# A two-block model in one kernel: first weight units in halves, products of zeros at the start, the linear attention's decayed keys computed first

## The reference, cut to what matters

```python
n = rms_norm(h, attn_norm)                       # 512 x 1024
z = n @ w_in
gq, gk, gv, g_low, g_r, c_q, c_kv, k_r = split_cols(z, IN_SPLITS)
log_a = log_sigmoid(g_low @ gla_gate_w2 + gla_gate_b) / 16
# linear attention: 4 heads, 64 keys and 128 values wide, chunks of 64 tokens
def step(state, inp):
    qi, ki, vi, gi = inp
    b = cumsum(gi, axis=2); b_last = b[:, :, -1:, :]
    o_inter = (qi * exp(b)) @ state
    decay = exp(where(causal, b_t - b_s, -inf))
    scores = einsum('bhtk,bhsk,bhtsk->bhts', qi, ki, decay)
    k_dec = ki * exp(b_last - b)
    state = state * exp(b_last) + k_dec.T @ vi
    return state, o_inter + scores @ vi
# softmax attention: 8 heads, queries and keys 96 wide, values 64, query blocks of 128, block-causal
q_m = rms_norm(rms_norm(c_q) @ mla_w_uq); kv = rms_norm(c_kv) @ mla_w_ukv   # rotary part, norms
o_m = mla_attention(q_m, k_m, v_m)
h = h + concat([o_g, o_m]) @ w_out
# then the MLP, a gated projection, and a second block (pooling, two gated FFNs with a short
# convolution, a 16-head banded attention); none of it is touched
```

## Time and profile before

| what | value |
|---|---|
| median of 3 runs | 1713.98 us (1710.64 to 1714.53) |
| the profiled execution | 1710.77 us, its span 1709.0 us |
| PE busy | 1667.6 us (98% of the span) |
| DVE, ACT, POOL busy | 955.7, 610.6, 120.9 us |
| mean granted TensorE clock | 0.990 |

### The profile page before, as it was taken

How to read it: one execution, slowest core, us unless ns; L and a number is a source line. 1 busy time by engine, 2 the same in 40 slices (tenths; PEclk the granted TensorE clock), 3 DMA queues, 4 the chain that set the end, 5 groups by cost and what they waited for, 6 DMA issues and landing times.

```text
span 1709.0 us, 19162 instructions
## 1 busy us (share of the span) xinstructions
PE 1667.6 (98%) x8098; PEld 1348.7 (79%) x8098; DVE 955.7 (56%) x1409; ACT 610.6 (36%) x851; POOL 120.9 (7%) x103
## 2 busy tenths in 40 slices
PE   7898899999999999999999999999999999999999
PEld 5785678888888888888888888877766888888887
DVE  4767756534343465847646546655655477356453
ACT  4346533423232333523322222445655433222221
POOL 1110010000000001500000000221200200000000
PEclk9899899999999999999999999999999999999999
DMA  5220003735353622122322313322221132322221
GB/s 177 99 99 1 1 26 114 116 123 88 124 88 104 119 101 97 51 74 99 123 82 93 121 69 105 99 97 75 84 97 38 49 123 100 119 77 99 99 80 68
DMA packets 26038, 153.84 MB, mean 90 GB/s; under 512 B 3360, under 2 KB 4528, under 8 KB 9952
## 3 DMA queue, kind: packets, MB, share of 16 engines
q1 hardware_dynamic: 24048, 146.83, 24.1%
q0 software_dynamic: 1328, 4.86, 4.9%
q10 hardware_dynamic: 576, 0.92, 0.2%
HBM read 147.88 MB, written 4.72 MB: 89 GB/s over the span
## 4 chain that ended last, share of the span: by engine, by line
PE 92%; DVE 5%; ACT 2%; issue 0%; DMA 0%; ACTq 0%
PE bank L517 24%; PE bank L519 24%; PE bank L518 24%; PE bank L523 4%; PE bank L525 3%; PE bank L524 3%; PE bank L1097 1%; PE bank L1119 1%; PE bank L1106 1%; DVE WL L1516 1%; PE bank L705 1%; PE bank L743 1%; ACT WH L1163 1%; ACT tmp L1300 1%; PE bank L726 0%; PE bank L983 0%
## 5 line engine op out<-in xcount | busy, mean ns | idle before, releaser
L517 PE MATMUL bank<-AH,WH 128*128 128x512 f32 (+1 forms) x1152 | 453.0, 393 | 12.3 <-DVE WL L1516 12.3
L518 PE MATMUL bank<-AL,WH 128*128 128x512 f32 (+1 forms) x1184 | 462.7, 391 | 0.0
L519 PE MATMUL bank<-AH,WL 128*128 128x512 f32 (+1 forms) x1152 | 449.9, 391 | 0.0
L1516 DVE TENSOR_TENSOR WL<-RAW,WH 128x2048 fp32r<-128x2048 f32 (+1 forms) x136 | 307.2, 2261 | 180.3 <-ACT WH L1163 180.3
L1163 ACT ACTIVATE WH<-RAW 128x2048 fp32r<-128x2048 f32 (+1 forms) x136 | 253.8, 1868 | 259.8 <-PE bank L519 238.7
L517 PEld LDWEIGHTS bank<-AH,WH 128*128 128x128 f32 (+1 forms) x1152 | 216.7, 188 | 60.7 <-DVE WL L1516 14.2
L518 PEld LDWEIGHTS bank<-AL,WH 128*128 128x128 f32 (+1 forms) x1184 | 222.9, 188 | 48.1 <-issue 1.8
L519 PEld LDWEIGHTS bank<-AH,WL 128*128 128x128 f32 (+1 forms) x1152 | 216.8, 188 | 46.5 <-issue 0.6
L517 PE MATMUL bank<-HH,WH 128*128 128x512 f32 x608 | 239.6, 394 | 0.0
L519 PE MATMUL bank<-HH,WL 128*128 128x512 f32 x608 | 238.4, 392 | 0.0
L518 PE MATMUL bank<-HL,WH 128*128 128x512 f32 x608 | 236.0, 388 | 0.0
(11 more groups left out here) (278 smaller groups left out, 1781.5 us busy)
## 6 DMA issues: line engine op xcount, KB each, us to landing
RAW<-in_W SPq DMA_DIRECT2D x125, 1024.0 KB, 4.8
RAW<-in_W SPq DMA_DIRECT2D x10, 768.0 KB, 4.3
ev_scratch<-ev POOLq DMA_DIRECT2D x16, 160.0 KB, 7.5
Gb<-ev_scratch SPq DMA_DIRECT2D x16, 128.0 KB, 2.9
out<-X SPq DMA_DIRECT2D x8, 256.0 KB, 2.0
Gb<-ev_scratch SPq DMA_DIRECT2D x16, 112.0 KB, 2.6
X<-in_XT SPq DMA_DIRECT2D x5, 256.0 KB, 7.7
X<-in_XT ACTq DMA_DIRECT2D x3, 256.0 KB, 7.1
```

The lines of the kernel that those rows point to most:

```text
L517: e.matmul(o, a, h, start=first, stop=False)
L518: e.matmul(o, a, l, start=False, stop=False)
L519: return e.matmul(o, c, h, start=False, stop=last)
L1516: e.tensor_tensor(k.WL[u % NW][:, 0:n], k.RAW[RAW_OF[u]][:, 0:n], k.WH[u % NW][:, 0:n].bitcast(F), SUB).then_inc(*WLO.mark(u))
```

## The change

- Units 0 and 1 are loaded and split in two halves of their columns each (pieces 0 to 3 and 4 to 7); the first products wait for the first halves only. All of `X` is loaded by SP; ScalarE's queue has the parameters and the first half of unit 0. The squares of the first norm come later in ScalarE's and VectorE's order.
- TensorE starts with 14 matmuls on 128 columns of zeros, which VectorE writes first. ScalarE makes a copy of four of these zeros before it waits for data.
- ScalarE copies the values (`vm`) before the split of unit 6 and before the last two squares; VectorE and ScalarE take their `fill` items accordingly, VectorE's split of unit 6 moves ahead of four items.
- In the loop, the decayed keys are made first (`last`, `kdec`), transposed in steps 1 and 2 and copied there; the 14 level items follow two steps later than before. `keep` takes item i - 4 and is the first thing that VectorE does in a step. `between` is gone: the decayed queries get a buffer of their own (`qd`) and are made in steps 16 and 17. The states are TensorE's in steps 17 and 18, the first of the two VectorE chains is in step 18. GpSimd's clearing of `kt` is gone.
- `kd` and `qd` lie in slot 0 of `WH`, so ScalarE splits unit `wout 2` only after the linear attention's outputs (`og`) are done. `attended(m)` uses the banks 3, 2, 0, 1.

```diff
@@ -231,7 +232,8 @@
-    k.kd = a.over("kd", [P, 4, 256], qm_at)
+    k.kd = a.over("kd", [P, 4, 256], wh_at + slot * UE * 4)
+    k.qd = a.over("qd", [P, 2, S], wh_at + slot * UE * 4 + 4 * 256 * 4)
@@ -283,12 +285,19 @@
+    k.half_in = [semaphore(f"half_in{i}") for i in range(2)]
+def half_of(k, u, x):
+    n = PLAN[u][2] // 2
+    return [z[u][:, x * n:x * n + n] for z in (k.RAW, k.WH, k.WL)] + [k.W[u, :, x * n:x * n + n]]
@@ -555,7 +564,7 @@
-        w.wait_ge(WLO(0), DVE("al", 0, c))
+        w.wait_ge(WLO(0) if c > 3 else WLO("half", 0), DVE("al", 0, c))
@@ -566,7 +575,7 @@
-        w.wait_ge(WLO(1), DVE("al", 0, c))
+        w.wait_ge(WLO(1) if c > 3 else WLO("half", 1), DVE("al", 0, c))
@@ -574,6 +583,9 @@
+    w.wait_ge(DVE("still"))
+    for _ in range(14):
+        e.matmul(bank[7][:, 0:P], k.rb[:, 0:P], k.rb[:, 0:P], start=True, stop=True)
@@ -693,6 +705,24 @@
+    def states(j):
+        bs = ((2, 7), (0, 1))[j]
+        for c in (0, 2, 4, 6, 1, 3, 5):
+            b = bs[c % 2]
+            r0 = 64 * (c % 2)
+            if c < 2:
+                w.wait_ge(*free[b])
+            for hh in range(2):
+                h = 2 * j + hh
+                t = e.matmul(bank[b][64 * hh:64 * hh + 64, (c // 2) * P:(c // 2 + 1) * P],
+                             k.kd[r0:r0 + 64, c // 2, j * P + 64 * hh:j * P + 64 * hh + 64],
+                             k.gv[r0:r0 + 64, c // 2, h * GV:(h + 1) * GV], start=True, stop=True, skip_group_check=True)
+            if c in (5, 6):
+                t.then_inc(*MM.mark("state", j, c % 2))
+        free[bs[0]], free[bs[1]] = [DVE("state", j, 6)], [DVE("state", j, 5)]
@@ -732,8 +762,15 @@
-        if 0 <= u < 14:
-            lv, j = levels[u]
+        if u in (0, 1):
+            b = (7, 3)[u]
+            w.wait_ge(DVE("kdec", u), *free[b])
+            for r in range(NT):
+                t = e.transpose(bank[b][:, r * P:(r + 1) * P], k.kt[:, u, r * P:(r + 1) * P], ident)
+            t.then_inc(*MM.mark("kturn", u))
+            free[b] = [ACT("kd", u)]
+        elif 2 <= u < 16:
+            lv, j = levels[u - 2]
@@ -745,43 +782,23 @@
-        elif u in (14, 15):
-            j = u - 14
...
-    for j in range(2):
-        w.wait_ge(ACT("kd", j), DVE("gv", 3))
...
+        elif u in (16, 17):
+            states(u - 16)
-        w.wait_ge(WLO(u), *free[m % 4])
+        b = (3, 2, 0, 1)[m % 4]
+        w.wait_ge(WLO(u), *free[b])
...
@@ -799,7 +816,7 @@
+                t = e.matmul(bank[ob[hh]][:, cs], k.ST[rows, j, c - 1, :], k.qd[rows, j, cs], start=False, stop=True,
@@ -1181,19 +1198,33 @@
+    def half_split(u, x):
+        raw, h, _, _ = half_of(k, u, x)
+        w.wait_ge(loaded(k, u) if x else (k.half_in[u], 16))
+        e.activation(h, raw, AF.Copy).then_inc(*(WHI.mark(u) if x else WHI.mark("half", u)))
+    def load_half(u, x):
+        raw, _, _, src = half_of(k, u, x)
+        e.dma_start(raw, src).then_inc(*((k.raw_full[u], 16) if x else (k.half_in[u], 16)))
-    for c in (1, 4, 6):
-        e.dma_start(X[:, c, :], k.XT[:, c, :]).then_inc(k.x_in[c], 16)
+    load_half(0, 0)
+    w.wait_ge(DVE("still"))
+    e.activation(k.m4[:, :], k.rb[:, 0:4], AF.Copy)
-        if c == 1:
-            split(0)
-        if c == 3:
-            split(1)
-        if c:
-            square(0, c - 1, X[:, c - 1, :])
-    square(0, 7, X[:, 7, :])
+        if c == 0:
+            half_split(0, 0)
+        elif c == 3:
+            half_split(1, 0)
+        elif c == 5:
+            half_split(0, 1)
+        if c > 3:
+            square(0, c - 4, X[:, c - 4, :])
+    half_split(1, 1)
+    for c in range(4, 8):
+        square(0, c, X[:, c, :])
@@ -1228,12 +1259,12 @@
-    fill(4)
-    split(6)
+    fill(2)
-    fill(2)
+    split(6)
+    fill(4)
@@ -1284,7 +1315,9 @@
-    w.wait_ge(DVE("scan", 1))
+    for j in range(2):
+        w.wait_ge(DVE("last", j))
+        e.activation(k.dd[:, j, :], k.dd[:, j, :], AF.Exp, scale=1.0 / 16).then_inc(*ACT.mark("elast", j))
@@ -1304,25 +1337,19 @@
-        if 0 <= u and u + 2 < 14:
-            lv, j = levels[u + 2]
+        if 2 <= u < 14 and levels[u][0]:
+            lv, j = levels[u]
-        if u in (13, 14):
-            j = u - 13
-            w.wait_ge(DVE("scan", j))
+        if u in (0, 1):
+            w.wait_ge(MM("kturn", u), MM("gv", 1, 3))
+            e.activation(k.kd[:, :, u * P:(u + 1) * P], bank[(7, 3)[u]][:, :].rearrange("p (q n) -> p q n", q=4), AF.Copy).then_inc(
+                *ACT.mark("kd", u))
+        if u in (14, 15):
+            j = u - 14
-            w.wait_ge(DVE("last", j))
-            e.activation(k.dd[:, j, :], k.dd[:, j, :], AF.Exp, scale=1.0 / 16).then_inc(*ACT.mark("elast", j))
-            w.wait_ge(DVE("kdec", j))
-            e.activation(k.dd[:, j, :], k.gb[:, j, :], AF.Exp, scale=1.0 / 16).then_inc(*ACT.mark("efirst", j))
-        if u in (14, 15):
-            j = u - 14
-            w.wait_ge(MM("kturn", j), MM("head", 0, 7))
-            e.activation(k.kd[:, :, j * P:(j + 1) * P], bank[7][:, :].rearrange("p (q n) -> p q n", q=4), AF.Copy).then_inc(
-                *ACT.mark("kd", j))
-    split(UNIT["wout", 2])
+            e.activation(k.qd[:, j, :], k.gb[:, j, :], AF.Exp, scale=1.0 / 16).then_inc(*ACT.mark("efirst", j))
@@ -1335,6 +1362,7 @@
+    split(UNIT["wout", 2], MM("og", 3))
@@ -1547,16 +1575,26 @@
+    def half_split(u, x):
+        raw, h, l, _ = half_of(k, u, x)
+        w.wait_ge(WHI(u) if x else WHI("half", u))
+        e.tensor_tensor(l, raw, h.bitcast(F), SUB).then_inc(*(WLO.mark(u) if x else WLO.mark("half", u)))
+    e.memset(rb[:, 0:P], 0.0).then_inc(*DVE.mark("still"))
-        if c == 1:
-            split(0)
-        if c == 3:
-            split(1)
-        if c > 2:
-            add_square(0, c - 2)
-    add_square(0, 6)
+        if c == 0:
+            half_split(0, 0)
+        elif c == 3:
+            half_split(1, 0)
+        elif c == 5:
+            half_split(0, 1)
+        if c > 4:
+            add_square(0, c - 4)
+    half_split(1, 1)
+    for c in range(4, 7):
+        add_square(0, c)
@@ -1678,9 +1716,10 @@
-        fill(1)
-    fill(2)
+        if q < 2:
+            fill(1)
+    fill(4)
@@ -1739,9 +1778,7 @@
-        w.wait_ge(ACT("decay", lv, j), POOL("kt0"))
-        if lv > 1:
-            w.wait_ge(MM("level", lv - 1, j, 1))
+        w.wait_ge(ACT("decay", lv, j), MM("level", lv - 1, j, 1) if lv > 1 else MM("kturn", j))
@@ -1753,21 +1790,29 @@
-        if lv > 1:
-            w.wait_ge(DVE("decayed", lv - 1, j))
-        w.wait_ge(DVE("scan", j))
+        w.wait_ge(DVE("decayed", lv - 1, j) if lv > 1 else DVE("kdec", j))
-    def between(j):
+    def last(j):
-        w.wait_ge(DVE("decayed", 6, j))
+        w.wait_ge(DVE("scan", j))
-        w.wait_ge(ACT("elast", j), MM("level", 6, j, 1))
-        e.tensor_tensor(k.kt[:, j, :], k.gk[:, j, :], k.dd[:, j, :], MUL).then_inc(*DVE.mark("kdec", j))
-        w.wait_ge(ACT("efirst", j))
-        e.tensor_tensor(k.qt[:, j, :], k.gq[:, j, :], k.dd[:, j, :], MUL).then_inc(*DVE.mark("qdec", j))
+    def chain(j):
+        bs = ((2, 7), (0, 1))[j]
+        for c in range(7):
+            o = bank[bs[c % 2]][:, (c // 2) * P:(c // 2 + 1) * P]
+            w.wait_ge(MM("state", j, 0), MM("state", j, 1)) if c else w.wait_ge(MM("state", j, 0))
+            if c == 0:
+                w.wait_ge(MM("head", 0, 7))
+                t = e.tensor_copy(k.ST[:, j, 0, :], o)
+            else:
+                w.wait_ge(DVE("state", j, c - 1), ACT("el", j))
+                t = e.scalar_tensor_tensor(k.ST[:, j, c, :], k.ST[:, j, c - 1, :], k.el[:, j, c:c + 1], o, MUL, ADD)
+            t.then_inc(*DVE.mark("state", j, c))
@@ -1780,7 +1825,13 @@
+    for j in range(2):
+        last(j)
+        if i == 18:
+            chain(0)
+        if 0 <= i - 4 < 14:
+            keep(*levels[i - 4])
@@ -1798,34 +1849,27 @@
-        if 0 <= i - 2 < 14:
-            keep(*levels[i - 2])
-        if 0 <= u and u + 1 < 14:
-            decayed(*levels[u + 1])
-        if 0 <= u and u + 2 < 14:
-            decay(*levels[u + 2])
-        if u in (13, 14):
-            between(u - 13)
-    for j in range(2):
-        for c in range(7):
...
+        if 2 <= u and u - 1 < 14:
+            decayed(*levels[u - 1])
+        if 1 <= u < 14:
+            decay(*levels[u])
+        if i in (0, 1):
+            w.wait_ge(ACT("elast", i), MM("gv", 1, 3))
+            e.tensor_tensor(k.kt[:, i, :], k.gk[:, i, :], k.dd[:, i, :], MUL).then_inc(*DVE.mark("kdec", i))
+        if u in (15, 16):
+            j = u - 15
+            w.wait_ge(ACT("efirst", j))
+            e.tensor_tensor(k.qd[:, j, :], k.gq[:, j, :], k.qd[:, j, :], MUL).then_inc(*DVE.mark("qdec", j))
+    chain(1)
@@ -2130,8 +2174,6 @@
-    w.wait_ge(MM("gv", 1, 3))
-    e.memset(k.kt[:, :, :], 0.0).then_inc(*POOL.mark("kt0"))
@@ -2213,13 +2255,19 @@
-    load_x(0)
-    load(0)
-    load_x(2)
-    load_x(3)
-    load(1)
+    def load_half(u, x):
+        raw, _, _, src = half_of(k, u, x)
```

(63 more changed lines are left out.)

1 line of the change is left out of this document (added).

## The result

The changed kernel takes 1689.05 us in the median (1685.93 to 1690.75, 4 runs) against 1713.38 of the kernel before in the same session: a ratio of 0.9852, 95% interval 0.9836 to 0.9868. A second set of four runs gave 1686.28 (1685.82 to 1691.29), 0.9839 (0.9819 to 0.9858). The median of all eight is 1687.2; forecast were 1688, and a range from 1678 to 1702. The profiled execution took 1685.93 us, its span 1684.1, so 24.9 less than the span before; the sum of the forecast was 24.5.

What follows compares the result with a forecast made beforehand. PE was taken as the bound, with time to win only where it stands or runs at half clock in the first 225 us. 4.8 + 8.2 + 11.5 = 24.5 us off 1710.8 gives 1686.3, forecast as 1688; range 1678 to 1702.

Steps and rivals of the forecast that it cites:

- The start: Up to the first norm: first product 3.0 us earlier plus 1.8 for the clock, 4.8 us won, between 3.0 and 5.8.
- The clock: At the start: products of zeros bring the high clock sooner; 1.8 us counted, bounds 0 and 2.8, as a gap follows.
- The value copies: Before the loop: no PE wait for `vm`, no half clock behind; 9.0 less 0.8 for late splits, 8.2 us won.
- The loop: All three parts of the loop together: 7.5 + 1.6 + 2.4 = 11.5 us won, kept between 4 and 19.
- Steps 4 to 14: Middle of the loop: `keep` first, VectorE bounds next; 57.0 us become 49.5, 7.5 won, between 2 and 12.7.
- Ahead of them: Loop before step 4: decayed keys go in front, wide masks and first levels move back; 1.6 us won.
- Behind them: Loop's end: `between` and PE's wait for `keep` go, other work comes in; 2.4 us won, between 0 and 5.6.
- two waits of 2.4 us: Steps 4 to 14: VectorE's waits that stay, added to its 43.2 us busy time, 48.0 in all.
- Behind the loop: Later `wout 2` and `wout 3` splits still fit by 0.8 us, nothing counted; rival, 4 us lost, chance 0.04.
- The lock in turns: Rival, loop: PE and VectorE wait on each other through `keep` and level; 32 us lost, 1731 us, chance 0.03.
- That the loop gives nothing: Rival: VectorE binds the loop as before in another order; 13.0 us won in all, 1699.5 us, chance 0.14.
- PE does not bind it yet: Rival judged: PE binds the loop at full clock, 8 us more, 32 in all, 1680 us, chance 0.10.

Runs made afterwards that it cites:

- keep_late: Changed kernel with `keep` put back behind the maxima and the bias in VectorE's step; 1697.05 us, ratio 0.9895.
- keep_first_old: Kernel with the old loop but new start and value order, `keep` of item i - 2 moved first in VectorE's step; 1694.86 us, ratio 0.9884.
- no_zeros: Changed kernel without its 14 products of zeros; 1689.36 us, ratio 0.9849.
- two_queues: Changed kernel with pieces 1, 4 and 6 of `X` issued by ScalarE's queue again; 1686.86 us, ratio 0.983.
- ol_late_states: Changed kernel with the attention output's low part behind VectorE's decay operations and TensorE's states brought forward; 1679.83 us, ratio 0.9793.
- hold15: Changed kernel with 8 unit-matrix products, into a bank nobody reads, ahead of the level of step 15; 1687.96 us, ratio 0.9849.

## Why the prediction was right, step by step

**The start.** First product forecast at 8.4 us, measured 8.20: 3.2 us for 3.0. The clock was put at 1.8 us, for a gap that "can go either way". It did both: 2.8 (26.5 to 23.8) in one profile of the changed kernel, 1.2 (to 25.3) in the other. Without zeros 0.9 come by themselves, as the clock rises after nine products instead of 14. The start gave 6.0 and 4.3 us for 4.8. That the early table load is hidden is right, but it was given no price; it is worth 0.1 to 0.7 us.

**The value copies.** Forecast 9.0 less 0.8 for late splits; measured 8.6 between the two profiles (14.55 less 5.96) and 9.1 when undone alone. The waits on the splits of units 7 and 8 did not come: the 0.8 us should not have been taken off.

**The loop.** Steps 4 to 14: 49.5 us forecast, 48.9 and 52.3 measured. Its mechanism, `keep` off the way of PE's level, is shown from both sides by keep_late and keep_first_old. Ahead of them 1.6 us were forecast and 4.2 measured: VectorE is busy 9.17 us there for 12.70 before, since the wide masks and first levels have left these steps (the place of `keep` plays no part: keep_late takes 13.1 us too); that this outweighs the decayed keys so far was missed. Behind them 2.4 won were forecast, and 1.9 lost: the term with the wrong sign. Where the clock held (no_zeros, two_queues) the stretch takes 15.5 us, 1.4 less than before; the other 3.3 are half clock after the stand in step 15, and the second profile of the changed kernel has them too (18.8). The forecast counted two waits of 2.4 us for ScalarE's copy as VectorE's alone. It didn't follow them to PE's level in the step behind, nor to the clock: waits of PE on `keep` under 2 us were forecast and 4.4 measured, and an idle gap of 2 to 3 us that stays in the loop and pulls the clock down, which the forecast named as a sign of being wrong, is there in step 15. In all the loop gave 10.3 us in the first profile (91.1 to 80.8) and 6.9 in the second, for 11.5.

**Behind the loop.** VectorE's split of `wout 2` begins at 217.87 us, in old times 242.8, and that of `wout 3` ends at 229.1, in old times 254.0:

```profile
217.87 2.29 DVE L1544 TENSOR_TENSOR WL<-RAW,WH 128x2048 fp32r<-128x2048 f32 x1 [2.36 <-ACT WH L1180]
...
226.82 2.29 DVE L1544 TENSOR_TENSOR WL<-RAW,WH 128x2048 fp32r<-128x2048 f32 x1 [0.60 <-ACT WH L1180]
```

Both are as forecast, and no wait of PE follows.

**The rivals.** The lock in turns is out: VectorE waits 0.9 us in all for PE's levels. That the loop gives nothing is out too, and PE does not bind it yet; ol_late_states shows how near that is, with PE busy 44.6 of 45.6 us in steps 4 to 14. The sum came out because terms of both signs missed (in the first profile +1.2 at the start, +0.4 at the values, +2.6, +0.6 and -4.3 in the three parts of the loop).

## What to carry to other kernels

When two engines serve each other in turns, put what the other waits for first in the step, and an operation that waits for a third engine last; follow each such wait into the next step of the engine that sets the end. Price a stand of TensorE of 1 to 3 us twice, once as time and once as a chance of half clock behind it, even for a short one: the stand of 1.1 us in step 11 was followed by half clock in nine profiles of nine. Fill it with work that is due anyway: products for nothing gave no measurable gain here (hold15), the states ahead of a level did, once the other stands were short (ol_late_states). An execution or two is too little to judge edits of 2 us: compare the same stretch in several traces.
